# A 128-partition two-block transformer kernel: first-use normalisation of the HGRN stage moved into that stage, and the low parts of one projection's weights moved to GpSimd

## What is computed

```python
def conv_ffn(h):                       # first block; D = 1024, hidden 2816
    p = h @ ffn_w_up                   # 1024 -> 5632 columns
    p = causal_conv3(p) + ffn_conv_b   # per column, three taps
    a, b = split(p)
    return (silu(a) * b) @ ffn_w_down

# second block, layer 1 (HGRN)
hn_l = modulate(rms_norm_2(h,  norm_mix_w[1]), sh1_l, sc1_l)   # 512 latent tokens
hn_c = modulate(rms_norm_2(hc, norm_mix_w[1]), sh1_c, sc1_c)   # 256 context tokens
z_fw, z_bw, v = split(h @ w_in[:, 2*W:])       # latent and context
q, gate       = split(h @ w_in[:, :2*W])       # latent only
# f = lb + (1-lb)*sigmoid(z); chunked scans in both directions, 8 heads
```

## Time and profile before

| | us |
|---|---|
| median of 3 runs (lowest, highest) | 3899.34 (3898.07, 3904.71) |
| the profiled execution, its own time | 3900.96 |
| the span of its trace | 3898.9 |
| TensorE busy | 3349.1 |
| VectorE busy | 1635.9 |
| ScalarE busy | 1125.3 |
| GpSimd busy | 497.3 |

### The profile page before, as it was taken

How to read it: one execution, slowest core, us unless ns; L and a number is a source line. 1 busy time by engine, 2 the same in 40 slices (tenths; PEclk the granted TensorE clock), 3 DMA queues, 4 the chain that set the end, 5 groups by cost and what they waited for, 6 DMA issues and landing times. The chain is left out here.

```text
span 3898.9 us, 49072 instructions
## 1 busy us (share of the span) xinstructions
PE 3349.1 (86%) x19354; PEld 2484.8 (64%) x19354; DVE 1635.9 (42%) x2526; ACT 1125.3 (29%) x1694; POOL 497.3 (13%) x366
## 2 busy tenths in 40 slices
PE   7688856797698889988868788999996999989998
PEld 5365521365455567766747667888654888847877
DVE  5433359522222457743155533222002788724332
ACT  2311323221311232223255533222002455413321
POOL 0000035000000110003302212000002222200001
PEclk9799877896599999999989888999998999989999
DMA  3266110121023112212100001111111111212222
GB/s 131 94 239 238 44 46 1 37 76 41 1 86 119 44 65 86 86 62 100 44 27 1 1 22 44 65 65 58 45 60 55 70 62 66 76 65 78 95 81 81
DMA packets 30423, 268.43 MB, mean 69 GB/s; under 512 B 2848, under 2 KB 5280, under 8 KB 10144
## 3 DMA queue, kind: packets, MB, share of 16 engines
q1 hardware_dynamic: 30240, 265.88, 18.9%
HBM read 261.68 MB, written 4.19 MB: 68 GB/s over the span
## 5 line engine op out<-in xcount | busy, mean ns | idle before, releaser
L595 PE MATMUL banks<-normed_high,weights_high 128*128 128x512 f32 (+1 forms) x2272 | 856.0, 377 | 145.2 <-DVEq L547 91.3
L595 PE MATMUL banks<-normed_low,weights_high 128*128 128x512 f32 (+1 forms) x2272 | 846.2, 372 | 0.0
L595 PE MATMUL banks<-normed_high,weights_low 128*128 128x512 f32 (+1 forms) x2272 | 845.1, 372 | 0.0
L595 PEld LDWEIGHTS banks<-normed_high,weights_high 128*128 128x128 f32 x2272 | 436.6, 192 | 256.4 <-DVEq L547 107.2
L261 DVE TENSOR_TENSOR weights_low<-ring,weights_high 128x1024 fp32r<-128x1024 f32 (+1 forms) x239 | 324.0, 1356 | 653.8 <-ACTq L534 633.5
L532 ACT ACTIVATE weights_high<-ring 128x1024 fp32r<-128x1024 f32 (+1 forms) x239 | 278.3, 1164 | 804.5 <-PE banks L595 500.0
L595 PEld LDWEIGHTS banks<-normed_high,weights_low 128*128 128x128 f32 x2272 | 436.9, 192 | 74.1
L595 PEld LDWEIGHTS banks<-normed_low,weights_high 128*128 128x128 f32 x2272 | 437.6, 193 | 69.1
L564 POOL TENSOR_TENSOR latent_total<-latent_total,latent_square 128x512 f32<-128x512 f32 x42 | 77.1, 1837 | 1880.9 <-ACTq L517 1880.9
L595 PE MATMUL banks<-ffn_hidden,ring 128*128 128x256 f32 (+1 forms) x704 | 227.3, 486 | 1.1 <-PEq L152 1.1
L2788 PE MATMUL banks<-normed_high,hg_weights_high 128*128 128x512 f32 (+1 forms) x512 | 187.1, 366 | 30.4 <-POOL hg_weights_low L2749 30.4
(11 more groups left out here) (514 smaller groups left out, 4958.8 us busy)
## 6 DMA issues: line engine op xcount, KB each, us to landing
ring<-in_ffn_up SPq DMA_DIRECT2D x33, 2048.0 KB, 8.1
ring<-in_ada SPq DMA_DIRECT2D x48, 1024.0 KB, 5.1
ring<-in_ffn_down SPq DMA_DIRECT2D x24, 1408.0 KB, 6.0
ring<-in_hgrn SPq DMA_DIRECT2D x16, 1536.0 KB, 6.5
ring<-in_gates SPq DMA_DIRECT2D x6, 2048.0 KB, 8.0
ring<-in_wo SPq DMA_DIRECT2D x6, 2048.0 KB, 8.2
ring<-in_w_rw SPq DMA_DIRECT2D x4, 2048.0 KB, 10.7
ring<-in_branch SPq DMA_DIRECT2D x3, 2048.0 KB, 8.0
```

Source lines behind the costliest of these rows:

```text
L595: mm = pe.matmul(ps[:, 0:y.shape[-1]], w, y, start=(kk == 0 and n == 0), stop=(kk == kt - 1 and n == len(pairs) - 1))
```

## The change

Three edits.

1. `linear` has a new argument `low_on`. Where it is "gpsimd", GpSimd writes the low part of each weight tile in place of VectorE; only the first block's `ffn_up` asks for it.
2. `apply_norms` and its stage are gone. `hgrn` places the same two norms itself (their roots and scaled tiles in buffers that the stage uses later), and each engine does its part at the head of its stream: ScalarE `high(0)`, `high(1)`, then `scalar_norms`; VectorE the latent columns ahead of `lower_bounds`; GpSimd `low(0)`, `low(1)`, then the context columns. TensorE waits in FORWARD of head 0 feature tile by feature tile.
3. `clear_keys` also waits until the context columns are normalised, since they are read from the space that it clears.

```diff
-           weights_move=False, keep_free=0, sums=(), norms=(), fetch=None):
+           weights_move=False, keep_free=0, sums=(), norms=(), fetch=None, low_on="vector"):
...
+                    prepare = {"scalar": high, low_on: low}.get(name) if split else None
+                    steps = len(parts) * sum(p for p, o in zip(per, on) if o == name) + (tiles if prepare else 0)
...
-            if "vector" in on or split:
+            if "vector" in on or split and low_on == "vector":
                 block.vector(emptier("vector"))
+            if split and low_on == "gpsimd":
+                block.gpsimd(emptier("gpsimd"))
...
             linear(k, "ffn_up", [H.operand(LAT)], conv, per=[3, 3, 6, 6], beside=(silu, 2),
-                   more={"squashed": FT}, norms=[lead])
+                   more={"squashed": FT}, norms=[lead], low_on="gpsimd")
...
-            apply_norms(k, [modulated(H.at, 1, 0, 1), modulated(H.at, 1, 0, 0)])
-            hgrn(k, H, OH)
+            hgrn(k, H, OH, lambda c, **how: modulated(H.at, 1, 0, c, **how))
...
+                low(0)
+                low(1)
+                context.by_scaler(e)
+                for j in range(2, NT):
                     low(j)
...
                         for kk in range(DT):
+                            if h == 0 and j == FORWARD:
+                                pe.wait_ge(norms[part].ready.sem, norms[part].ready.at(kk + 1))
...
                 high(0)
+                high(1)
+                scalar_norms(k, e, norms, summed)
                 a.wait_ge(back.sem, back.at(1))
                 a.activation(LT[:, 1:3, :], LT[:, 1:3, :], ACT.Exp).then_inc(done.sem, 1)
-                high(1)
...
                     v.wait_ge(n["residual_parked"].sem, n["residual_parked"].at(16))
+                    v.wait_ge(context.ready.sem, context.ready.at(DT))
                     v.memset(KI[:], 0.0).then_inc(e.sem, e.tick())
...
+                latent.by_scaler(e)
                 lower_bounds()
                 clear_keys()
                 decays(0)
```

More of the change, by code:

```diff
@@ L608, in run @@
                     e = k.engine(eng, name + "_steps", ends)
-                    steps = len(parts) * sum(p for p, o in zip(per, on) if o == name) + (tiles if split else 0)
+                    prepare = {"scalar": high, low_on: low}.get(name) if split else None
+                    steps = len(parts) * sum(p for p, o in zip(per, on) if o == name) + (tiles if prepare else 0)
                     if name == "scalar" and beside is not None:
                         steps += beside[1]
-                    prepare = high if name == "scalar" else low
                     if sums and name == "scalar":
                         eng.preload_act_table_set("natural_log_exp_and_others")
-                    if split:
+                    if prepare:
                         prepare(e, (0, None, 0))
@@ L623, in run @@
                         for j, ahead in lay.tiles_ahead(s, i):
-                            if ahead is not None and split:
+                            if ahead is not None and prepare:
                                 prepare(e, ahead)
@@ L653, in linear @@
     lay.end()
[L656 to L685, removed]
 def inverse_root(e, out, mean, scale, eps):
@@ L2646, in heads_norm_rope, with hgrn @@
             ends.update(keys_rounded=2, logs_ready=n, squared=n, squares_summed=n, rooted=n, operands_ready=n, products_ready=n, products_taken=n)
-def hgrn(k, H, OH):
+def hgrn(k, H, OH, norm_of):
     C2 = 2 * C
@@ L2717, in hgrn @@
         TRI = sb("triangles", [P, C2 + C])
+        flat = SS[:].rearrange("p a c n -> p (a c n)")
+        latent = norm_of(1, root=AT[:].rearrange("p c n -> p (c n)"), scaled=[SQ[:], A2[:].rearrange("p c n -> p (c n)")])
+        context = norm_of(0, root=flat[:, 0:CTX], scaled=[flat[:, CTX:2 * CTX], flat[:, 2 * CTX:3 * CTX]])
+        norms = (latent, context)
+        for r in norms:
+            r.place(k, s)
+        summed = k.count("squares_summed")
         fetched = k.count("small_weights_loaded")
@@ L2759, in add @@
                     g.sem_inc(n["scores_added"].sem, 1)
-                for j in range(NT):
+                low(0)
+                low(1)
+                context.by_scaler(e)
+                for j in range(2, NT):
                     low(j)
@@ L3171, in hgrn @@
                         residual_parked=16, squashed=1, operands_ready=1, small_weights_loaded=16)
+            for r in norms:
+                r.ends(ends)
     k.used += 2 * heads
```

## The result

The changed kernel takes 3862.1 us (median of 4 runs, 3858.3 to 3873.27) against 3899.52 (4 runs, 3898.07 to 3904.71) of the kernel before: ratio 0.9906, 95% interval 0.9893 to 0.9919, so 36.7 us saved, with 31.6 and 41.7 as ends. The forecast was 3865 us, 34.6 saved. The profiled execution took 3858.3, its span is 3856.2.

The account below looks back on a forecast made before the run. TensorE was taken to bound the kernel, losing time to late low parts in `ffn_up` and idling during `apply_norms`. 3900.96 - 26.7 (`ffn_up`, 28.6 - 1.9) - 7.9 (HGRN) = 3866.4, less 1.6 to the median: 3864.8 us, range 3857 to 3877.

Parts of the forecast that it names:

- What bounds.: TensorE, busy 86% of the span, loses time in `ffn_up` in 20 waits for VectorE's low parts, 22.3 us in all.
- Stalls: 28.6 us: In the first `ffn_up`, 20 stalls of TensorE cost 28.6 us, 1.43 each, and all go.
- The low part's margin, "1.3 us": In `ffn_up`, GpSimd's low part is ready 1.3 us before TensorE wants it, taking 2.48 us per instruction.
- What GpSimd takes from VectorE: In `ffn_up`, GpSimd holds only VectorE's product, copy and hidden low part, 0.8 us a long tile, at no cost.
- It is the order that is late, not the engine.: In `ffn_up`, VectorE is busy only 191.80 of 267 us but makes the low part after six evacuation instructions.
- The head of `ffn_up`, 1.9 us: At the stage's start, slower first low parts and a held VectorE scaling cost 1.9 us, bounds 0.9 and 3.4.
- HGRN, 7.9 us: Norms inside `hgrn` remove a stage boundary and follow the pattern of `q2`: 7.9 us saved, bounds 5.5 and 10.
- The costs at nothing: In `hgrn`, delayed exponential and sigmoid, `clear_keys`, parking transfer, slot loads and head 0's wait all cost nothing.
- Bank readers: Rival in `ffn_up`: GpSimd also holds VectorE's instructions that read a bank, so `ffn_up` gains nothing, 3893 us; 7 in 100.
- The late low part: Rival in `ffn_up`: GpSimd takes over 3.8 us from the rounding's end, all 43 tiles stall, slower than before; 3 in 100.
- HGRN did not save little: Rival: norms inside `hgrn` save only -1 to 4 us, total 3872 us; 8 in 100.
- No half of the stalls stayed: Rival in `ffn_up`: half the stalls stay because ScalarE's rounding queues behind a late silu, 3879 us; 4 in 100.

Follow-up runs that it names:

- Experiment 3: Changed kernel, but TensorE waits in FORWARD of head 0 for all 16 normalised feature tiles at once: 3875.19 us (one run).
- 11: The changed kernel measured again, unaltered: 3867.26 us, ratio 0.9911 against the kernel before.
- experiments 1: Kernel before with only the low parts of the first `ffn_up` moved to GpSimd, `apply_norms` kept: 3875.06 us, ratio 0.9931.
- experiment 8: Changed kernel, but VectorE makes HGRN's first two low parts ahead of the latent norm: 3868.77 us, ratio 0.9909 against the kernel before.
- experiment 6: Changed kernel, but GpSimd repeats half of each low part in `ffn_up`: 3869.37 us (one run).
- experiment 7: Changed kernel, but GpSimd makes each low part of `ffn_up` twice: 3930.76 us (one run).
- experiment 4: Changed kernel, but VectorE makes `ffn_up`'s low parts two tiles ahead, in the middle of its evacuation: 3881.14 us, ratio 0.995 against the kernel before.
- experiment 2: Kernel before with only the norms moved into the HGRN stage, `ffn_up`'s low parts left on VectorE: 3892.61 us, ratio 0.998.

## Why the prediction was right, point by point

**What bounds.** Right: the 20 waits were the loss, and all went.

**"Stalls: 28.6 us."** 30.0. The sum by starts was 30.1; I took 1.5 off for a stretch at the lower clock that I thought would stay, and in the profiled execution it didn't. In experiments 3 and 11 the same stage lost 2.9 there, in experiments 1 and 8 nothing, so the subtraction was fair as a mean and no term of the edit. Without the 1.6 us that the clock cost before, the stalls were 28.4. That the total came out this close (34.6 forecast, 36.7 measured) is in part luck: the ends of the measured saving are 10 us apart, and the changed kernel's second profile has `ffn_up` 2.9 us longer.

**The low part's margin, "1.3 us".** 1.4 by experiment 6; with 2.6 us more a tile the whole gain was gone (experiment 7). The GpSimd instruction took 2343 to 2408 ns, nearer to the least of rows 5 than to the median that I used.

**"What GpSimd takes from VectorE": 0.8 us a long tile, two or three instructions held.** Over-sized: only the product is held, by 0.28 us in the median and 0.57 at most. It cost nothing, as predicted.

**"It is the order that is late, not the engine."** Half wrong, though the sum didn't need it. VectorE's mean load allows the low parts, and another order alone won back 10.6 of the 28.1 us of the stage (experiment 4), but two long evacuations side by side with a low part in each outlast TensorE's tiles. Moving the low part away took both the order and this burst off the path. Of the kernels run here, the Trainium skill's rule (GPSIMD Engine Reference, 4.1 Engine selection) that elementwise work belongs on VectorE would have chosen a slower one: on GpSimd one low part takes 2.40 us in place of 1.23, and the stage is 17.6 us shorter than in experiment 4.

**The head of `ffn_up`, 1.9 us.** 1.88: second tile at 24.93 against 23.05. The 0.7 of the held scaling is there (2.36 against 1.65 for two).

**HGRN, 7.9 us.** 8.57. The start of the context was 0.3 later than worked out (GpSimd's pair took 5.14, not 4.68, since VectorE's first scaling came in between), the way from there to BACKWARD 25.44 in place of the 26.45 of `q2`: 0.6 less up to the last latent feature, which I didn't follow up, and 0.4 less in the context's matmuls, where the clock rose earlier. Experiment 3 shows that the overlap is the gain.

**The costs at nothing** (lower bounds, first sigmoid, cleared keys, slots): nothing of it shows. `clear_keys` began 1.3 us later than worked out (31.1 us after ScalarE's first instruction), and TensorE's one long wait in head 0 is 3.29 us as before.

**Rivals.** Bank readers are not held (749 to 752 ns). The late low part is a real limit, 1.4 us away. HGRN did not save little. No half of the stalls stayed; the way named for it, a rounding queued behind a late silu, shows in experiment 7, where VectorE is held for longer.

## What to carry to other kernels

Where an engine with much idle time is the one waited for, look at the longest stretch of its order between two signals, not at its load: work that is released early but queued behind it belongs in front of it or on another engine, even one that takes twice as long. Work out that other engine's margin from the release to the need; here it was 1.4 us of 5.4, and 2.6 us more a tile turned 37 us saved into some 30 lost. Read small edits in the pieces of the trace they touch: these repeated within 0.3 us where the clock was the same (it moved one by 2.9), while untouched pieces moved by up to 9.

## What the runs showed of the chip that I had not expected

The clock behind the same gap is not the same twice. In the changed kernel's profile TensorE stood for 3.22 us ahead of the second tile of `ffn_up` and went on at 2.4 GHz; in its repetition it stood for 3.23 us and then ran 14 matmuls at 1.2 GHz (0.43 us apart), which cost 2.9 us (236.70 against 233.82). In the kernel before it fell at 1430.0, 1.3 us after a gap of 2.06. In the first head of HGRN, behind the same wait of 3.29 us, the granted clock was 0.56 in one kernel and 1.00 in the other (experiment 2). At the stage's start the clock took back 0.8 of the 1.8 us by which experiment 8 had made the chain earlier. A gain of 1 or 2 us at the head of a stage can be lost there whatever the edit does.

GpSimd and VectorE take turns by whole instructions, in both directions: VectorE's scaling waited 1.9 us for the end of a GpSimd low part (2.61 in place of 0.75), and the GpSimd pair took 0.46 longer for the VectorE instruction between.
